# The down weights' fourth chunk split into high and low parts as well, in a mixture-of-experts decoder trunk

## What is computed

```python
scores = jax.nn.sigmoid((t @ router_w).astype(jnp.float32))
...                          # best group of 4 experts, then the best 2 in it
gates = jnp.sum(jax.nn.one_hot(eidx, N_EXPERTS, dtype=jnp.float32) * w[..., None], axis=-2)
out = jnp.zeros_like(t)
for e in range(N_EXPERTS):   # 16
    hid = jax.nn.silu(t @ w_gate[e]) * (t @ w_up[e])     # 1024 -> 512, twice
    out = out + gates[:, e:e + 1] * (hid @ w_down[e])    # 512 -> 1024
```

## Time and profile before

| | us |
|---|---|
| median of 3 executions | 1571.74 |
| lowest and highest | 1570.76 and 1576.95 |
| the profiled execution | 1572.55 |
| its span, from the first to the last instruction | 1570.7 |

### The profile page before, as it was taken

The page is one execution under the profiler, slowest core; times in us unless marked ns, Lnnn a source line. Parts: engine busy times, 40 slices in busy tenths (PEclk is TensorE's granted clock), DMA queues, the critical chain, the costliest instruction groups (busy, mean ns, idle before and its releaser), DMA issues. The chain is left out here.

```text
span 1570.7 us, 17335 instructions
## 1 busy us (share of the span) xinstructions
PE 1379.1 (88%) x6443; PEld 1072.3 (68%) x6443; DVE 1097.4 (70%) x1295; ACT 721.0 (46%) x983; POOL 184.8 (12%) x268
## 2 busy tenths in 40 slices
PE   7499988886989999999818998889698999999991
PEld 3377775665777777777516777756487777777771
DVE  0577775665469888888557786655656788888873
ACT  1422433454137666666323343344513566666650
POOL 0000013500111000000020000252001000001002
PEclk9699998687999999999958999887799899999996
DMA  9536552321279999999365374242208699999955
GB/s 350 203 107 222 198 212 87 121 94 68 93 272 346 405 401 401 402 389 381 122 225 177 126 282 178 95 151 92 94 28 321 248 387 399 395 404 406 401 196 187
DMA packets 95260, 379.54 MB, mean 242 GB/s; under 512 B 5897, under 2 KB 8695, under 8 KB 85704
## 3 DMA queue, kind: packets, MB, share of 16 engines
q1 hardware_dynamic: 71592, 308.82, 52.0%
q0 software_dynamic: 15264, 55.63, 9.1%
q10 hardware_dynamic: 8320, 13.96, 2.5%
HBM read 345.58 MB, written 32.82 MB: 241 GB/s over the span
## 5 line engine op out<-in xcount | busy, mean ns | idle before, releaser
L1051 PE MATMUL ps<-mod_rounded,work_rounded 128*128 128x512 f32 x340 | 139.2, 410 | 1.1 <-DVE work_rounded L1892 1.1
L1053 PE MATMUL ps<-mod_rounded,work_rounded 128*128 128x512 f32 x340 | 135.2, 398 | 0.0
L1758 DVE TENSOR_TENSOR ring_rounded<-ring,mod_rounded 128x2048 fp32r<-128x2048 f32 (+1 forms) x54 | 103.0, 1932 | 24.3 <-ACT mod_rounded L1342 24.3
L1758 DVE TENSOR_TENSOR work_rounded<-work,mod_rounded 128x2048 fp32r<-128x2048 f32 (+1 forms) x48 | 91.4, 1932 | 33.2 <-ACT mod_rounded L1342 33.2
L1052 PE MATMUL ps<-ring_rounded,work_rounded 128*128 128x512 f32 x288 | 113.9, 396 | 0.0
L1438 DVE SCALAR_TENSOR_TENSOR gain<-ring,csil,gain 128x512 f32<-128x512 f32 x134 | 101.8, 760 | 3.8 <-DMA ring<-in_ada_w 0.7
L1052 PE MATMUL ps<-work_rounded 128*128 128x512 f32 x256 | 101.3, 396 | 0.0
L810 PE MATMUL ps<-ring_rounded,actT_rounded 128*128 128x512 f32 (+1 forms) x256 | 93.5, 365 | 0.0
L1342 ACT ACTIVATE mod_rounded<-ring 128x2048 fp32r<-128x2048 f32 (+1 forms) x54 | 86.2, 1632 | 0.0
L1206 ACT ACTIVATE work<-ps 128x512 f32<-128x512 f32 (+1 forms) x48 | 26.3, 548 | 129.8 <-PE ps L810 77.5
L1051 PE MATMUL ps<-actT_rounded,work_rounded 128*128 128x512 f32 x204 | 81.0, 397 | 0.0
(11 more groups left out here) (335 smaller groups left out, 3580.6 us busy)
## 6 DMA issues: line engine op xcount, KB each, us to landing
ring<-in_ada_w SPq DMA_DIRECT2D x38, 1024.0 KB, 5.3
ring<-in_moe_w_gate SPq DMA_DIRECT2D x18, 2048.0 KB, 10.3
ring<-in_moe_w_up SPq DMA_DIRECT2D x18, 2048.0 KB, 10.8
ring<-in_moe_w_down SPq DMA_DIRECT2D x18, 2048.0 KB, 11.6
work<-in_moe_w_gate SPq DMA_DIRECT2D x16, 2048.0 KB, 10.5
work<-in_moe_w_up SPq DMA_DIRECT2D x16, 2048.0 KB, 11.3
work<-in_moe_w_down SPq DMA_DIRECT2D x16, 2048.0 KB, 11.9
expert_rows<-work POOLq DMA_DIRECT2D x34, 512.0 KB, 8.3
```

Of the source, the lines that this page charges most:

```text
L1051: pe.matmul(ps[j][:, :], xl, hi, start=k == 0, stop=False)
L1053: mm = pe.matmul(ps[j][:, :], xh, hi, start=False, stop=k == KD - 1)
L1758: v.tensor_tensor(slots_r[3 * odd + j][:, 512 * k0:512 * k1], slots[3 * odd + j][:, 512 * k0:512 * k1], buf.bitcast(F32), ALU.subtract).th ...
```

## The change

All four chunks of the down weights are split now. The f32 matmul of line 1074 goes and chunk 3 gets three rounded ones, so that a half is 12 matmuls. ScalarE makes a third high part in each turn, in chunks 0 and 1 of `actT` (1024 columns), for the last tile in chunks 2 and 3; VectorE makes a third low part. The hidden columns are written by one copy of four chunks, and their low part has four chunks. TensorE's wait for the low parts moves between the matmuls of the first half, one for each part. For the first tile, the third high part waits for the router's last result (`pos_dn`). `w12` and `wsum` move from `route` into `sml`.

```diff
-    hT_r = view(18432, 3, P, of=work_r)
-    hT_lo = view(19968, 3, P, of=work_r)
+    hT_r = view(18432, 4, P, of=work_r)
+    hT_lo = view(19968, 4, P, of=work_r)
...
-    DOWN_SPLIT = 3
-    down_hi_parts = [(0, 2, biasm_r[:, :, :].rearrange("p a b -> p (a b)")), (2, 3, gain_r[:, :])]
-    down_hi_last = [(0, 2, mod_r[:, 2048:4096]), (2, 3, mod_r[:, 4096:5120])]
+    down_hi_parts = [(0, 2, biasm_r[:, :, :].rearrange("p a b -> p (a b)")), (2, 3, gain_r[:, :]),
+                     (3, 4, actT_r[:, 0:2, :].rearrange("p a b -> p (a b)"))]
+    down_hi_last = [(0, 2, mod_r[:, 2048:4096]), (2, 3, mod_r[:, 4096:5120]),
+                    (3, 4, actT_r[:, 2:4, :].rearrange("p a b -> p (a b)"))]
...
-    w12 = route[:, 896:904].rearrange("p (a t) -> p a t", a=2)
-    wsum = route[:, 904:908]
+    w12 = sv(824, 8).rearrange("p (a t) -> p a t", a=2)
+    wsum = sv(832, 4)
...
-                    pe.wait_ge(d_lo, 2 * e + 2)
-                    w = slots[n].rearrange("p (k n) -> p k n", k=4)
                     lo_ = slots_r[n].rearrange("p (k n) -> p k n", k=4)
                     for b in range(2):
                         cols = slice(512 * b, 512 * b + 512)
-                        pe.matmul(ps[6 + b][:, :], hT3, w[:, 3, cols], start=True, stop=False)
-                        for k0, k1, buf in down_high(e):
+                        for m, (k0, k1, buf) in enumerate(down_high(e)):
+                            if b == 0:
+                                pe.wait_ge(d_lo, 3 * e + (m + 1))
                             hi_ = buf.rearrange("p (k n) -> p k n", k=k1 - k0)
                             for k in range(k0, k1):
-                                pe.matmul(ps[6 + b][:, :], hT_lo[:, k, :], hi_[:, k - k0, cols], start=False, stop=False)
+                                pe.matmul(ps[6 + b][:, :], hT_lo[:, k, :], hi_[:, k - k0, cols], start=k == 0, stop=False)
                                 pe.matmul(ps[6 + b][:, :], hT_r[:, k, :], lo_[:, k, cols], start=False, stop=False)
                                 mm = pe.matmul(ps[6 + b][:, :], hT_r[:, k, :], hi_[:, k - k0, cols],
-                                               start=False, stop=k == DOWN_SPLIT - 1)
+                                               start=False, stop=k == 3)
...
                 def h_out(e):
                     a.wait_ge(ht_ps, e + 1)
-                    a.activation(hT_r, ps[4][:, 0:384].rearrange("p (k n) -> p k n", k=3), ACT.Copy)
-                    a.activation(hT3, ps[4][:, 384:512], ACT.Copy).then_inc(ht_ev, 1)
+                    a.activation(hT_r, ps[4][:, :].rearrange("p (k n) -> p k n", k=4), ACT.Copy).then_inc(ht_ev, 1)
...
-                    for k0, k1, buf in down_high(e):
+                    for m, (k0, k1, buf) in enumerate(down_high(e)):
+                        if e == 0 and m == 2:
+                            a.wait_ge(pos_dn, 2)
                         a.activation(buf, slots[3 * odd + 2][:, 1024 * k0:1024 * k1], ACT.Copy).then_inc(d_hi, 1)
...
-                    v.tensor_tensor(hT_lo, ps[4][:, 0:384].rearrange("p (k n) -> p k n", k=3), hT_r.bitcast(F32),
+                    v.tensor_tensor(hT_lo, ps[4][:, :].rearrange("p (k n) -> p k n", k=4), hT_r.bitcast(F32),
                                     ALU.subtract).then_inc(hl_lo, 1)
...
-                        v.wait_ge(d_hi, 2 * e + (m + 1))
+                        v.wait_ge(d_hi, 3 * e + (m + 1))
```

More of the change, by code:

```diff
@@ L213, in trunk @@
     chosen = view(4096, 2 * T, D)
-    hT_r = view(18432, 3, P, of=work_r)
-    hT_lo = view(19968, 3, P, of=work_r)
+    hT_r = view(18432, 4, P, of=work_r)
+    hT_lo = view(19968, 4, P, of=work_r)
     hT = view(18432, 4, P)
-    hT3 = view(18432 + 384, P)
     xeT_r = view(14336, KD, P, of=work_r)
```

## The result

| | before | after |
|---|---|---|
| median of the runs | 1571.74 us (9 runs, 1564.6 to 1577.0) | 1562.79 us (9 runs, 1557.5 to 1570.5) |
| ratio, 95% interval | | 0.9942 [0.9914, 0.9970] |
| profiled execution: time, span | 1572.55, 1570.70 | 1561.08, 1559.4 |
| one steady turn of the expert stage | 18.36 | 17.93 |
| last down product of the first and the second layer: its start, counted from the start of the last tile's gate products; from its first to its last matmul's start | 19.12; 5.72 and 5.74 | 19.85; 6.95 and 6.96 |

The changed kernel is 8.95 us faster by the medians; 9.4 were forecast (1562.3). The sum comes out, but two of its terms do not: a gain of 1.4 us in each layer, which stood among the rivals only, and a loss of 1.6 us, which stood nowhere. They nearly cancel, so the closeness of the sum is in part luck.

A forecast was written before the change was run, and what follows sets the result against it. TensorE was taken to set the 18.36 us turn. Per layer, 15 x 0.35 = 5.25 less 0.49 gave 4.76, or 9.5 us over two layers: 1562.3 us against the 1571.74 median, range 1558.5 to 1567.

The forecast's parts named there:

- TensorE's part: Down product per expert: 24 rounded matmuls at 0.230 take 5.52 us instead of 5.87, a gain of 0.35 us.
- the rival with 0.2333 in the down product: Down product's matmuls step at 0.2333 us, gaining 0.27 per expert; time 1564.6 us; chance 0.12.
- VectorE's, ScalarE's and the loads' parts: Steady turn: VectorE's added 1.28 us, ScalarE's extra 0.95 us copy and the weight loads fit existing gaps and cost nothing.
- a cover of 7.5 us: Down weights land 7.5 us before ScalarE opens them; a load lag growing to 5.3 us would stay inside that.
- The gate step: Rival: gate and up products step at 0.231 us, 0.11 more gained a turn, 3.1 us in all; 1559.2 us; chance 0.12.
- The tail: Last tile of each layer: VectorE's third subtract is on the path; the tail grows by 0.49 us.
- the forecast 0.84: Last tile: TensorE's wait for hidden-low ends at 1532.74 instead of 1531.90, behind the third subtract and wider hidden-low subtract.
- 5.82 with the f32 matmuls replaced: Last tile: from TensorE's restart to the last scaling takes 5.82 us, the former 6.17 less 0.35.
- The sum: Per layer 15 down products x 0.35 = 5.25, less 0.49 for the tail, 4.76; two layers 9.5 us.

The follow-up runs named there:

- its tail shortened: Changed kernel with the last tile's first down copy waiting for the gate product alone and its subtract moved ahead of `hidden`: 1558.34 us, ratio 0.9926.
- its tail overlapped as well: Tail-shortened kernel plus own hidden columns for the last tile, transposed between halves of the preceding down product, and one output scaling moved later: 1558.93 us, ratio 0.9918.
- the kernel with shorter down products: Kernel before with the down product's f32 matmul left out and nothing in its place, so the fourth chunk is not computed: 1521.88 us, ratio 0.9677.

## Why the prediction was right, and which steps were not

**TensorE's part: right in kind, by two errors that nearly cancel.** The step is 0.231, the lower of the two values that were kept; the rival with 0.2333 in the down product falls. But 24 equal steps left out that the first one, behind the transposes, is 0.32: the product takes 5.63 us where 5.52 were forecast, and gains 0.24 instead of 0.35. The other 0.08 came from the transposes ahead of it, which the forecast took as fixed. Together 0.32 a turn.

**VectorE's, ScalarE's and the loads' parts: right.** +1.28 a turn on VectorE; its wait fell to 0.04 (0.06 forecast), the second stayed at 0.85. ScalarE's wait ahead of the SiLU fell to 1.24 (0.9 forecast). The loads' lag did not grow at all: the share of 1.00 had read as if there were no reserve, yet 413 GB/s were delivered, and only a turn of 17.38 or less would have met the bound. Here the prediction was sure of "no cost" for a weaker reason, a cover of 7.5 us, and was right. Its 7.1 MB a turn came from the lowest of the steady turns, 388 GB/s; the mean is 7.4, so the need was larger than it worked out; the turn of 17.38 leaves a reserve of 0.55 us.

**The gate step: counted as a rival at 0.12, and it came true besides the forecast.** Of the 15 turns ahead of the tail in each layer, the first two lost about 0.33 each and the other 13 lost 0.43; the 0.10 to 0.11 more gives 1.4 us a layer. The prediction had read both steps in the earlier trace rows and took the present one as fixed. The run with the f32 matmul moved shows that the order of the matmuls can change it; that with the f32 matmul kept shows that the added work of VectorE and ScalarE does not; that with no f32 matmul, which steps at 0.2333, shows that it is neither the f32 matmul as such nor what stands next to the down product. What picks the step is open.

**The tail: the step that failed.** Its first half was right: the last down product starts 0.73 later after the last gate products' start, which is the forecast 0.84 less 0.1 for the quicker step of those gate products. Its second half, "5.82 with the f32 matmuls replaced", took the full clock for granted over a standstill that its own numbers made 1.2 us longer: 0.84 for the later start and 0.35 for the shorter down product ahead of it (1.15 measured, 1.39 to 2.54). The product went from 5.7 to 6.96 us instead of to 5.4, 1.56 a layer. Eight steps at 0.42 instead of 0.23 are 1.5 of it. It was mis-sized in rate, not in work.

**The sum.** For the first layer: 15 turns lost 6.21 us together (275.24 to 269.03), where 5.25 were forecast, and the tail grew by 0.73 + 1.23 = 1.96, where 0.49 was: 4.25 gained, against 4.76. The second layer's steady turns and tail are the same. Two layers give 8.5, and the medians differ by 8.95. The spans of the profiled executions differ by 11.3, because the first two turns of the second layer, partly at half clock before (15.74 and 19.85 us), ran whole after (14.63 and 17.98). That is 3.0 us, about 2.6 of it beyond the usual shortening; another execution of the changed kernel has 15.38 us for the first of these turns, and that with its tail shortened 15.69 and 19.59, so I take it as no part of the change. The profiled span alone would have overstated the gain.

The best kernels here that compute the whole result are the changed one with its tail shortened, 1558.34 us, 0.9926 [0.9898, 0.9954], and the one with its tail overlapped as well, 1558.93 us, 0.9918 [0.9885, 0.9950]; the time does not tell them apart.

## What to carry to other kernels

Where a change lengthens an idle time of TensorE on the path, read the granted clock of the work that comes after it: the price can be the idle time and a slower product behind it, and filler work that fits into the gap, or work brought forward out of it, takes the second back. A rate that differs between two stretches of the same kernel at the same clock is a quantity that a change can move, also one in another product; cost it at both values in the sum. And a DMA share of 1.00 is not a bound by itself: the bound is the rate at which the landing times begin to grow.

## What the runs showed of the hardware

Gate and up products of 128x512 rounded matmuls at the full clock have two steady steps, 0.2311 and 0.2333 us, and most turns of a layer have the same one. Moving one f32 matmul within another product changed it. Both steps occur with and without f32 matmuls in that product. The first rounded matmul behind the transposes steps at 0.31 to 0.32.

In the tail, TensorE's clock was granted at half (0.51 in the second layer's stretch, the 1.2 GHz level) for 3.4 us behind standstills of 2.54 and 2.22 us, in both layers and in each run that kept them; not behind 1.39 and 1.46, and not behind 2.65 in the kernel with shorter down products. At a layer's second tile it was half behind 1.21 and 0.54 us in one execution and whole behind the same two in another.

One core alone moved 420 to 423 GB/s over whole turns, mostly weights, and needed 17.38 us for what one turn moves. The DMA share read 1.00 or 1.01 at 388 GB/s as well as at 422.
